# Two-block cross-attention units with trailing value products, and pooling projections ahead of the second block's self-attention

## The chip, the cores and the metric

The kernel runs on one core of a Trainium2 chip. Five engines work side by side on their own instruction queues: TensorE (PE, matrix products; its weight loads are shown as PEld), VectorE (DVE), ScalarE (ACT), GpSimd (POOL) and SyncE (SP, which here only issues transfers). An engine takes its queue in order and waits on semaphores for the others. Matrix products are written to PSUM, which has eight banks of 128 x 512 fp32 numbers; everything else lies in SBUF. The metric is device time in microseconds (us), median of several runs.

## The reference, cut to what matters

Two transformer blocks run one after the other on a sequence of 512 rows of width 1024. Only the second block is touched. It computes:

```
for l in range(2):
    hn = rms_norm(h, norm_mix_g[l])
    if l == 0: h = h + even_mixer(hn, ...)      # differential attention + pooling
    else:      h = h + odd_mixer(hn, ...)       # gated convolution
    h = h + cross_attention(rms_norm(h, norm_xattn_g[l]), mem_n, wq[l], wkv[l], wo[l])
    h = h + sq_relu_mlp(rms_norm(h, norm_mlp_g[l]), w1[l], w2[l])
```

`even_mixer` projects `hn` to q, k, v and u. Four heads of causal differential attention, with two softmaxes each, `softmax(q1 k1) - lam * softmax(q2 k2)`, go through v and a norm. Four groups of u are pooled over 2, 4, 8 and 16 rows and pass through a 128 x 128 matrix each. `cross_attention` has four heads of width 256 against 256 memory rows, with `softmax(q k / 16) v`, and then `@ wo`.

## The kernel before, in words

Activations are held transposed, features on partitions, rows of the sequence along the free dimension. Each is kept as a pair hi/lo of the reduced-precision type fp32r (`P0H`, `P0L`, `P1H`, `P1L`; `MH`, `ML` for the memory), and so is each weight (`whi`, `wlo`). A big product is three passes, hi*hi, lo*hi and hi*lo (`gemm_fm`, L315, passes L325 to L327; `gemm_tm`, L335, passes L350 to L352). A weight chunk is loaded by SP into `raw`, rounded to `whi` by ScalarE (L180) and its rest put into `wlo` by VectorE (L171, 128 x 1024). The projections of a chunk of 128 output columns are 8 steps of 3 passes, one `yield` after each step.

The attention products are plain fp32, which PE runs as two passes each. A unit is one block of 128 query rows of one head (self-attention: two score maps). `attention` (L511) steps through units and issues four things for each:

- `scores`: q times k into PSUM (L525), then on VectorE the maximum (L534, or L542 together with the bias) and its negation, and on ScalarE the exponential into a tile `Tb`.
- `norm`: VectorE divides by the sum (and combines the two maps, L174).
- `turn`: PE transposes the probabilities (L588), ScalarE copies them from PSUM to `PTb`.
- `values`: PE multiplies v by `PTb` (L613) into an output bank. The last unit of a head ends with `done_pair`.

In round i, the order is `norm(i-1)`, `values(i-2)`, `scores(i)`, a pause, `turn(i-1)`, a pause. `drive(main, fill, num, den)` (L365) runs `main`, the attention, up to a pause and then takes on average num/den steps from `fill`, which holds big products that don't depend on it. So the order on every engine is fixed when the program is built: `fill` is what PE does while a unit's softmax is under way.

In the even mixer, all four query projections stand ahead of the attention. `fill_E` (L1201) has the four pooling projections (`project`), their mixes (`mix`) and the keys and values of the first cross-attention (`kv`, L1237), at 132/49 steps per pause. `project(g)` is evacuated by VectorE into `UP`; GpSimd makes 1 to 4 additions; a `rest` that VectorE does later (`waiting`) finishes it. In `kv` a key step is three passes of 256 columns and a value step six.

`cross` (L1320) computes the queries of head 0 and then runs 16 units, four per head. Its `fill` has the queries of heads 1 to 3 and, in layer 0 only, the second layer's `kv`. The steps per pause are 5 in layer 0 and 9/4 in layer 1. Then `xattn_wo` follows (`mixed`, L1307), 8 gemms that each need all four heads.

From the even mixer on there are three `Tb` tiles, two `PTb`, two score banks (`SB`), one bank for transposes, two output banks and three banks for big products.

Of the kernel before, what the change touches and what calls it, by code (L numbers as in the profile page):

```python
# [5 lines left out]
F32 = mybir.dt.float32  # L6
F32R = mybir.dt.float32r
ACT = mybir.ActivationFunctionType
ALU = mybir.AluOpType
# [132 lines left out]
def lay_out(nc, A, plan, T):  # L142
# [172 lines left out]
    def gemm_fm(src, w, parts, evac, N=512, last=True, n0=0):  # L315
# [3 lines left out]
        for n, (b, t) in enumerate(parts):  # L319
# [11 lines left out]
            yield  # L331
# [179 lines left out]
    def attention(units, done_pair):  # L511
# [3 lines left out]
        def scores(u):  # L515
# [13 lines left out]
            for j, ((bank, _), p) in enumerate(zip(banks, prods)):  # L529
# [3 lines left out]
                if u["kind"] == "plain":  # L533
                    o = op(DV, lambda e, mx=mx, bank=bank: e.reduce_max(mx, bank[:, 0:kl], axis=AX), p, sfree)  # L534
                elif u["kind"] == "forget":
# [12 lines left out]
                else:  # L548
                    o = op(DV, ts(nm, mx, -1.0, None, ALU.mult), o)
                src = bank[:, 0:kl] if u["kind"] == "plain" else t[:, 0:kl]  # L550
                x = op(AC, act(t[:, 0:kl], src, ACT.Exp, bias=nm, accum_out=l), o,
                       tfree if u["kind"] == "plain" else None)
                if u["kind"] == "plain":
                    SB.give(bank, x)
# [599 lines left out]
    for i in range(4):  # L1154
        w = Weight(chunk("ab_w_in", 0, halves(0), halves(128 * i, 1)))
        run(gemm_fm(P0, w, parts8(), to_rows(0.125, qE[:, i, :], tok, ("q", i))))
# [43 lines left out]

    def fill_E():  # L1201
        def project(g):
            w = Weight(chunk("ab_w_in", 0, halves(0), halves(1536 + 128 * g, 1)))
            yield from gemm_fm(P0, w, parts8(), pool_evac(g))

        def mix(g):
            w = Weight(chunk("pool_w", g, halves(0, 1), halves(0, 1)))

            def evac(bank, p):
                t, free = TMP.take()  # L1210
                o = op(DV, ts(t, bank, gcol("ps", g), None, ALU.mult), p, free)
                split_into(P1, 4 + g, t, o, give=t)
                return o

            assert P1.tok[g] is not None
            yield from gemm_fm(P1, w, [(0, g)], evac)

        for g in range(4):
            for n, _ in enumerate(project(g)):
                if n == 3 and g:  # L1220
                    waiting.pop(g - 1)()
                yield
            if g:
                yield from mix(g - 1)
        keys = kv(0)
        for n in range(12):
            if n == 7:
                waiting.pop(3)()
            next(keys)
            yield  # L1230
        yield from mix(3)
        yield from keys

# [3 lines left out]
    def kv(l, before=None):  # L1237

        kvt = kvtok[l]
        for h in range(4):  # L1240
            while before and not all("T" in u for u in before[4 * h:4 * h + 4]):
                yield
            for i in (2 * h, 2 * h + 1):
# [6 lines left out]
                yield from gemm_fm(MEM, w, parts8(), evac, N=256)  # L1250
            while before and not all("over" in u for u in before[4 * h:4 * h + 4]):
                yield
# [6 lines left out]
    for h in range(4):  # L1259
        for i in range(4):  # L1260
# [3 lines left out]
                qk=[tok[("q", h)], tok[("k", h)]],  # L1264
# [19 lines left out]
    def even_main():  # L1284
        yield from attention(eun, head_done)
# [18 lines left out]
    drive(even_main(), fill_E(), 132, 49)  # L1304
# [15 lines left out]
    def cross(l, gname):  # L1320
# [10 lines left out]
        un = []  # L1331
        for h in range(4):
            for i in range(4):
                un.append(dict(
                    kind="plain", len=256, pair=h, nout=2, first=i == 0, last=i == 3,
                    qk=lambda h=h: [tok[2 * h], tok[2 * h + 1], kvt[("k", 2 * h)], kvt[("k", 2 * h + 1)]],
                    mm=[[(qX[:, 2 * h + d, 128 * i:128 * i + 128], KT[:, 2 * h + d, :]) for d in range(2)]],
                    vtok=[kvt[("v", 2 * h)], kvt[("v", 2 * h + 1)]],
                    outs=[(d, 0, 128, 128 * i,
                           [VM[:, j, 256 * h + 128 * d:256 * h + 128 * d + 128] for j in range(2)], 0)  # L1340
                          for d in range(2)]))

        def done(u, banks, p):
            fr = []
            for d in range(2):
                m = 2 * u["pair"] + d
                a = op(AC, act(P1.hi[:, m, :], banks[d], ACT.Copy), p)
                o = op(DV, sub(P1.lo[:, m, :], banks[d], P1.hi[:, m, :].bitcast(F32)), a)
                P1.tok[m] = [a, o]
                fr.append(o)  # L1350
            return fr

        def fill():
            for h in range(1, 4):
                yield from qs(h)
            if l == 0:
                yield from kv(1, un)

        if l == 0:
            drive(attention(un, done), fill(), 5, 1)  # L1360
# [331 lines left out]
```

How the kernel before makes its waits and increments, by code:

```python
    def dma(self, eng, fn, sem, val, *deps):  # L93
        self.op(eng, lambda e: fn(e).then_inc(sem, 16), *deps)
        return Landed(sem, val)
# [9 lines left out]
    def play(self, eng, e):  # L105
        seen = {}
        for o in self.of[eng]:
            need = {}
            for d in o.deps:
                v = need.get(id(d.sem), (0, None))[0]
                need[id(d.sem)] = (max(v, d.val), d.sem)
            for k, (v, s) in need.items():
                if seen.get(k, 0) < v:
                    e.wait_ge(s, v)
                    seen[k] = v
            ins = o.fn(e)
            if o.sig:
                ins.then_inc(o.sem, 1)
# [23 lines left out]
def lay_out(nc, A, plan, T):  # L142
# [1348 lines left out]
    d, o = diagonal(RC[:, 0:4], rstd(NS[:, 0:4], o, RC[:, 0:4]))  # L1491
    bank, free = SB.take()
    p = op(PE, lambda e: e.matmul(bank, ones, d, start=True, stop=True), o, free, c_ones)
    row = op(AC, act(RB[:, :], bank, ACT.Copy), p)
    for n, m in enumerate((0, 5, 1, 2, 6, 3, 7, 4)):
        if m > 4:
            o = op(PO, mult(X[:, m, :], X[:, m, :], RB[:, :]), row, gained[m])
        else:
            o = op(DV, stt(X[:, m, :], X[:, m, :], gcol("last", m), RB[:, :], ALU.mult, ALU.mult), row)
        Q.dma(SP, lambda e, m=m: e.dma_start(A["outT"][:, m, :], X[:, m, :]), T["s_o"], 16 * (n + 1), o)
    op(SP, lambda e: e.wait_ge(T["s_o"], 128))
    return Q, used
```

## Time and profile before

| | |
|---|---|
| median of 3 runs | 2375.24 us (2373.6 to 2375.85) |
| the profiled execution | 2375.47 us, of which the span of instructions 2373.7 |
| PE busy | 2323.9 us, 98% of the span |
| VectorE, ScalarE, GpSimd busy | 56%, 36%, 1% |
| mean granted PE clock | 0.996 |

The span is the time from the first instruction to the last. A matrix product is pipelined: its recorded time includes its way through the array, so the next one starts before it ends, and the pace is read from start to start. A wait is shown as idle time behind a row, with what ended it.

### The profile page before, as it was taken

The numbers are of one execution on the slowest core, as the hardware profiler recorded it, in microseconds if no ns is written. First come the engines' busy times: TensorE is split into PE (matmuls) and PEld (weight loads), VectorE is DVE, ScalarE is ACT, GpSimd is POOL, SyncE is SP. The second block draws the span as 40 slices with busy tenths as digits, with TensorE's granted clock in tenths as the row PEclk, the third lists the DMA queues.
The fourth block names the chain that finished last, engine by engine and source line by source line (L and its number), as shares of the span: only waits on it lengthen the run. The fifth ranks groups of instructions, "written<-read, shape, count | busy, mean of one in ns | idle before, by whom it ended". The sixth has DMA issues, their size and how long they took to land.

```text
span 2373.7 us, 28772 instructions
## 1 busy us (share of the span) xinstructions
PE 2323.9 (98%) x11510; PEld 1875.8 (79%) x11510; DVE 1324.4 (56%) x2470; ACT 858.4 (36%) x1483; POOL 23.3 (1%) x21
## 2 busy tenths in 40 slices
PE   8999999999999999989999999999999989999997
PEld 6787778878777787878798888888888878888886
DVE  5855565556656657486545544444755545444444
ACT  4334443433444334254333432232322334332232
POOL 1000000000000000010000000000000000000000
PEclk9999999999999999999999999999999999999998
DMA  4322223322322233223233322223233213223221
GB/s 164 105 74 86 77 74 99 103 81 85 98 71 77 78 103 112 76 90 116 89 97 108 98 90 97 98 90 97 89 98 98 80 36 98 95 92 98 97 90 54
DMA packets 65417, 217.00 MB, mean 91 GB/s; under 512 B 8415, under 2 KB 9695, under 8 KB 65156
## 3 DMA queue, kind: packets, MB, share of 16 engines
q1 hardware_dynamic: 65284, 215.16, 28.6%
q8 instruction: 91, 1.49, 0.2%
q14 instruction: 42, 0.34, 0.0%
HBM read 207.78 MB, written 2.11 MB: 88 GB/s over the span
## 4 chain that ended last, share of the span: by engine, by line
PE 95%; DVE 3%; ACT 1%; issue 0%; DMA 0%; DVEq 0%; SPq 0%; ACTq 0%
PE ps L325 27%; PE ps L327 26%; PE ps L326 26%; PE ps L525 3%; PE ps L613 3%; PE ps L588 2%; PE ps L350 2%; PE ps L351 1%; PE ps L352 1%; DVE t_wlo L171 1%; PE ps L414 1%; DVE t_P0L L174 0%; ACT t_Tb L180 0%; PE ps L868 0%; PE ps L870 0%
## 5 line engine op out<-in xcount | busy, mean ns | idle before, releaser
L325 PE MATMUL ps<-t_P0H,t_whi 128*128 128x512 f32 x1664 | 676.8, 407 | 8.7 <-DVE t_P0L L174 8.6
L327 PE MATMUL ps<-t_P0H,t_wlo 128*128 128x512 f32 x1664 | 656.7, 395 | 0.0
L326 PE MATMUL ps<-t_P0L,t_whi 128*128 128x512 f32 x1664 | 655.0, 394 | 0.0
L180 ACT ACTIVATE t_whi<-t_raw 128x1024 fp32r<-128x1024 f32 (+2 forms) x396 | 404.7, 1026 | 384.4 <-PE ps L327 328.5
L171 DVE TENSOR_TENSOR t_wlo<-t_raw,t_whi 128x1024 fp32r<-128x1024 f32 (+2 forms) x396 | 469.5, 1188 | 11.4 <-ACT t_whi L180 6.3
L325 PEld LDWEIGHTS ps<-t_P0H,t_whi 128*128 128x128 f32 x1664 | 313.6, 188 | 102.2 <-issue 24.8
L327 PEld LDWEIGHTS ps<-t_P0H,t_wlo 128*128 128x128 f32 x1664 | 312.9, 188 | 73.1
L326 PEld LDWEIGHTS ps<-t_P0L,t_whi 128*128 128x128 f32 x1664 | 313.6, 188 | 67.6 <-issue 2.2
L325 PE MATMUL ps<-t_P1H,t_whi 128*128 128x512 f32 x900 | 354.6, 394 | 0.7 <-DVE t_P1L L171 0.7
L327 PE MATMUL ps<-t_P1H,t_wlo 128*128 128x512 f32 x900 | 354.8, 394 | 0.0
L326 PE MATMUL ps<-t_P1L,t_whi 128*128 128x512 f32 x900 | 354.2, 394 | 0.0
L325 PEld LDWEIGHTS ps<-t_P1H,t_whi 128*128 128x128 f32 x900 | 169.5, 188 | 41.0 <-DVE t_P1L L171 1.6
L327 PEld LDWEIGHTS ps<-t_P1H,t_wlo 128*128 128x128 f32 x900 | 169.1, 188 | 39.2
L326 PEld LDWEIGHTS ps<-t_P1L,t_whi 128*128 128x128 f32 x900 | 169.2, 188 | 39.0
L168 DVE TENSOR_TENSOR t_X<-ps,t_X 128x512 f32<-128x512 f32 x128 | 88.5, 692 | 163.4 <-PE ps L327 163.4
L180 ACT ACTIVATE t_TMP<-t_TMP 128x512 f32<-128x512 f32 x89 | 56.4, 633 | 280.5 <-DVE t_TMP L174 229.2
L174 DVE SCALAR_TENSOR_TENSOR t_TMP<-ps,t_RB 128x512 f32<-128x512 f32 x64 | 44.3, 692 | 178.4 <-PE ps L327 178.3
L180 ACT ACTIVATE t_Tb<-t_Tb,t_ST 128x128 f32<-128x128 f32 (+3 forms) x128 | 67.5, 528 | 208.2 <-DVE t_ST L177 208.2
L174 DVE SCALAR_TENSOR_TENSOR t_X<-ps,t_X 128x512 f32<-128x512 f32 x48 | 33.2, 692 | 112.1 <-PE ps L327 112.1
L180 ACT ACTIVATE t_P0H<-t_X,t_gv 128x512 fp32r<-128x512 f32 x56 | 40.0, 724 | 148.3 <-DVE t_X L174 136.2
L180 ACT ACTIVATE t_PTb<-ps 128x256 f32<-128x256 f32 (+3 forms) x176 | 63.4, 397 | 65.8 <-PE ps L588 65.6
L180 ACT ACTIVATE t_P1H<-t_TMP 128x512 fp32r<-128x512 f32 x89 | 56.3, 632 | 70.8 <-DVE t_TMP L165 47.7
(235 smaller groups left out, 2495.5 us busy)
## 6 DMA issues: line engine op xcount, KB each, us to landing
t_raw<-in_wts SPq DMA_DIRECT2D x364, 512.0 KB, 3.5
t_raw<-in_wts SPq DMA_DIRECT2D x16, 384.0 KB, 3.0
t_raw<-in_wts SPq DMA_DIRECT2D x4, 520.0 KB, 6.3
t_X<-in_xT SPq DMA_DIRECT2D x4, 512.0 KB, 6.3
t_raw<-in_wts SPq DMA_DIRECT2D x8, 256.0 KB, 2.7
outT<-t_X SPq DMA_DIRECT2D x8, 256.0 KB, 2.3
t_TMX<-t_TMX SPq DMA_DIRECT2D x28, 64.0 KB, 2.0
t_TMP<-t_TMX SPq DMA_DIRECT2D x24, 64.0 KB, 2.0
```

The source lines that it names most:

```text
L168: return lambda e: e.tensor_tensor(o, a, b, ALU.add)
L171: return lambda e: e.tensor_tensor(o, a, b, ALU.subtract)
L174: return lambda e: e.scalar_tensor_tensor(out=o, in0=a, scalar=s, in1=b, op0=f, op1=g)
L180: return lambda e: e.activation(o, a, f, **k)
L325: e.matmul(bank[:, 0:N], wh, xh, start=first, stop=False)
L326: e.matmul(bank[:, 0:N], wh, xl, start=False, stop=False)
L327: return e.matmul(bank[:, 0:N], wl, xh, start=False, stop=end)
L350: e.matmul(out, xh, wh, start=k == 0, stop=False)
L351: e.matmul(out, xh, wl, start=False, stop=False)
L525: i = e.matmul(bank[:, 0:kl], l, r, start=n == 0, stop=n == len(mm) - 1)
L588: i = e.transpose(bank[:, 128 * j:128 * j + 128], t[:, 128 * j:128 * j + 128], ident[:, :])
L613: i = e.matmul(o, vs[j], pts[n][:, 128 * j:128 * j + 128], start=j == 0, stop=j == nk - 1)
```

## The change

Three things are changed.

1. Cross-attention gets loops of its own. A unit is now two blocks of 128 queries of a head, so there are 8 units in a layer. One `reduce_max` over a 128 x 2 x 256 view serves both blocks, there are two exponentials of 256 columns, one division over 512 columns, four transposes into one bank, and value products with 256 moving columns. The order of a round is `norm(i-1)`, `scores(i)`, a pause, `values(i-2)`, `turn(i-1)`, a pause. In layer 1, `fill` also starts the first two gemms of `xattn_wo` on the heads that are done (parts 0 to 5), with empty steps between; these two are ended behind the loop. The rate there is 13/3 in place of 9/4. `kv(1)` waits for two units of a head where it waited for four.
2. `attention` takes `late_values`, which the even mixer sets: `values(i-2)` stands behind the first pause, right ahead of `turn(i-1)`. The other callers keep their order.
3. In the even mixer, the four pooling projections and query 0 run ahead of the attention, and queries 1 to 3 go into `fill_E`, which now holds queries, mixes and `kv(0)`. A key step of `kv` is six passes (`every=2`). The rate is 92/49.

```
-            yield
+            if n % every == every - 1:
+                yield
...
         for i in range(n + 2):
             if 1 <= i <= n:
                 norm(units[i - 1])
-            if i >= 2:
+            if i >= 2 and not late_values:
                 values(units[i - 2])
             if i < n:
                 scores(units[i])
             yield
             flush()
+            if i >= 2 and late_values:
+                values(units[i - 2])
             if 1 <= i <= n:
                 turn(units[i - 1])
             yield
...
+    for g in range(4):
+        for n, _ in enumerate(project(g)):
+            if n == 3 and g:
+                waiting.pop(g - 1)()
+    run(queries(0))
+    waiting.pop(3)()
+
     def fill_E():
+        yield from queries(1)
+        for g in (0, 2):
+            yield from mix(g)
+            yield from mix(g + 1)
+            yield from queries(2 + g // 2)
+        yield from kv(0)
...
-    drive(even_main(), fill_E(), 132, 49)
+    drive(even_main(), fill_E(), 92, 49)
...
+        def values(u):
...
+                for d in range(2):
+                    o = held[h][d][0][:, 256 * n:256 * n + 256]
+                    for j in range(2):
+                        c = 256 * h + 128 * d
+                        i = e.matmul(o, VM[:, j, c:c + 128], pt[:, 256 * j:256 * j + 256], start=j == 0, stop=j == 1)
...
+            for m in range(2):
+                open_.append(wo(m))
+            for parts, rest in ((range(0, 4), 1), (range(4, 6), 3)):
+                for g in open_:
+                    for k in parts:
+                        assert P1.tok[k] is not None
+                        next(g)
+                        for _ in range(1 + rest):
+                            yield
...
-            drive(attention(un, done), fill(), 9, 4)
-        run(mixed("xattn_wo", l, halves(0), 1.0, gname, P1))
+            drive(main(), fill(), 13, 3)
+        for g in open_:
+            run(g)
+        for m in range(len(open_), 8):
+            run(wo(m))
```

On PE, in the middle of the even mixer's attention, the order before was this (`t_ident` marks transposes, `t_PTb` value products, `t_MH` and `t_ML` the fill of `kv`; an x3 stands for three alike):

```order
L588 MATMUL ps<-t_ident,t_Tb 128x128 x3
L325 MATMUL ps<-t_MH,t_whi 128x256
L326 MATMUL ps<-t_ML,t_whi 128x256
L327 MATMUL ps<-t_MH,t_wlo 128x256
L325 MATMUL ps<-t_MH,t_whi 128x256
L326 MATMUL ps<-t_ML,t_whi 128x256
L327 MATMUL ps<-t_MH,t_wlo 128x256
L325 MATMUL ps<-t_MH,t_whi 128x256
L326 MATMUL ps<-t_ML,t_whi 128x256
L327 MATMUL ps<-t_MH,t_wlo 128x256
L613 MATMUL ps<-t_PTb,t_E_82 128x128 x3
L525 MATMUL ps<-t_E_82 128x128 x2
```

The value products of a unit follow its transposes after one pause. In the changed program the same engine and place read:

```order
L526 MATMUL ps<-t_E_82 128x128 x2
L325 MATMUL ps<-t_MH,t_whi 128x256
L326 MATMUL ps<-t_ML,t_whi 128x256
L327 MATMUL ps<-t_MH,t_wlo 128x256
L325 MATMUL ps<-t_MH,t_whi 128x256
L326 MATMUL ps<-t_ML,t_whi 128x256
L327 MATMUL ps<-t_MH,t_wlo 128x256
L608 MATMUL ps<-t_PTb,t_E_82 128x128 x3
L583 MATMUL ps<-t_ident,t_Tb 128x128 x4
```

The value products (x3) now belong to a unit whose transposes stand a whole round earlier, with another unit's scores between. At the end of the second layer's cross-attention, PE had this before, up to the last row ahead of `xattn_wo` (`t_KT` marks scores):

```order
L613 MATMUL ps<-t_PTb,t_VM 128x128 x4
L525 MATMUL ps<-t_KT,t_E_82 128x256 x2
L588 MATMUL ps<-t_ident,t_Tb 128x128 x2
L613 MATMUL ps<-t_PTb,t_VM 128x128 x4
L525 MATMUL ps<-t_KT,t_E_82 128x256 x2
L588 MATMUL ps<-t_ident,t_Tb 128x128 x2
L613 MATMUL ps<-t_PTb,t_VM 128x128 x4
L588 MATMUL ps<-t_ident,t_Tb 128x128 x2
L613 MATMUL ps<-t_PTb,t_VM 128x128 x4
```

There was no fill left. The changed program has, near the same place:

```order
L1392 MATMUL ps<-t_PTb,t_VM 128x256 x4
L1368 MATMUL ps<-t_ident,t_Tb 128x128 x4
L325 MATMUL ps<-t_P1H,t_whi 128x512
L326 MATMUL ps<-t_P1L,t_whi 128x512
L327 MATMUL ps<-t_P1H,t_wlo 128x512
L325 MATMUL ps<-t_P1H,t_whi 128x512
L326 MATMUL ps<-t_P1L,t_whi 128x512
L327 MATMUL ps<-t_P1H,t_wlo 128x512
L1342 MATMUL ps<-t_KT,t_E_82 128x256 x4
```

The six passes between are two steps of `xattn_wo`. On VectorE, where the even mixer's attention begins, the rows before are the evacuation of query 3 (into `t_E_82`), a clearing of `UP` and the first unit's softmax (L542):

```order
L174 SCALAR_TENSOR_TENSOR t_E_82<-ps,t_RB 128x512
L1159 MEMSET t_UP 128x3x16
L542 ISA t_Tb,t_ST<-ps,t_E_82 128x128
L542 ISA t_ST 128x1
L177 TENSOR_SCALAR t_ST<-t_ST 128x1
```

and in the changed program:

```order
L165 TENSOR_TENSOR t_UP<-ps,t_RB 128x512
L171 TENSOR_TENSOR t_wlo<-t_raw,t_whi 128x128
L174 SCALAR_TENSOR_TENSOR t_E_82<-ps,t_RB 128x512
L174 SCALAR_TENSOR_TENSOR t_TMP<-t_UP 128x496
L165 TENSOR_TENSOR t_UP<-t_UP,t_ic 128x16
L171 TENSOR_TENSOR t_TMP<-t_UP 128x16
L541 ISA t_Tb,t_ST<-ps,t_E_82 128x128
```

Query 0 is evacuated right ahead of the first softmax, and the end of pooling group 3, which waits for GpSimd, stands between.

## Rows read from the trace of the kernel before

**Rows 1.** The page's first part: busy time of each engine and instructions.

```profile
PE 2323.9 (98%) x11510; PEld 1875.8 (79%) x11510; DVE 1324.4 (56%) x2470; ACT 858.4 (36%) x1483; POOL 23.3 (1%) x21
```

**Rows 2.** Stretches: length, busy per engine, PEclk (granted clock), DMA share, GB/s.

```profile
972.40:994.70 22.30, 22.30 (x98) 17.88 (x96) 8.50 (x10) 4.45 (x5) 0.00 (x0) 1.00 0.24 78
994.70:1037.00 42.30, 40.00 (x200) 29.01 (x199) 36.74 (x111) 19.89 (x49) 11.54 (x10) 1.00 0.23 71
1037.00:1089.00 52.00, 44.54 (x323) 38.37 (x324) 40.01 (x127) 26.56 (x59) 1.12 (x1) 0.97 0.30 93
...
1245.00:1282.00 37.00, 34.04 (x266) 32.44 (x265) 18.97 (x43) 13.73 (x29) 0.00 (x0) 1.00 0.35 112
...
1931.90:1955.20 23.30, 14.98 (x90) 12.63 (x89) 7.80 (x25) 5.67 (x18) 0.00 (x0) 0.93 0.00 1
```

**Rows 3.** PE's waits from 1037 to 1089: total us, times, longest.

```profile
PE ps L613 <- ACT t_PTb L180: 4.5, 4, 2.2
PE ps L588 <- DVE t_Tb L174: 3.5, 3, 2.5
```

**Rows 4.** PE's timeline in that stretch: start us, us, engine, line, [idle before <-releaser].

```profile
1056.19 1.13 PE L525 MATMUL ps<-t_E 64*128 64x512 f32 x4
...
1058.89 0.28 PE L326 MATMUL ps<-t_ML,t_whi 128*128 128x256 f32 x1
...
1059.73 0.28 PE L327 MATMUL ps<-t_MH,t_wlo 128*128 128x256 f32 x1
1062.20 1.15 PE L613 MATMUL ps<-t_PTb,t_E 128*128 128x128 f32 x6 [2.20 <-ACT t_PTb L180]
```

**Rows 5.** ScalarE's timeline in the same microseconds.

```profile
1058.27 0.73 ACT L180 ACTIVATE t_Tb<-t_Tb,t_ST 128x512 f32<-128x512 f32 x1 [2.78 <-DVE t_ST L177]
...
1059.79 1.99 ACT L180 ACTIVATE t_whi<-t_raw 128x1024 fp32r<-128x1024 f32 x2
1061.68 0.47 ACT L180 ACTIVATE t_PTb<-ps 128x384 f32<-128x384 f32 x1
```

**Rows 6.** VectorE's timeline in the same microseconds.

```profile
1059.61 2.48 DVE L171 TENSOR_TENSOR t_wlo<-t_raw,t_whi 128x1024 fp32r<-128x1024 f32 x2
...
1062.84 0.75 DVE L174 SCALAR_TENSOR_TENSOR t_Tb<-t_Tb,t_ST 128x512 f32<-128x512 f32 x1
```

**Rows 7.** PE's timeline, end of the second layer's cross-attention.

```profile
1931.97 1.10 PE L613 MATMUL ps<-t_PTb,t_VM 128*128 128x128 f32 x8
1932.91 1.03 PE L525 MATMUL ps<-t_KT,t_E 128*128 128x256 f32 x4
1933.77 0.38 PE L588 MATMUL ps<-t_ident,t_Tb 128*128 128x128 f32 x2
1935.51 1.16 PE L613 MATMUL ps<-t_PTb,t_VM 128*128 128x128 f32 x8 [1.36 <-ACT t_PTb L180]
...
1955.19 0.48 PE L325 MATMUL ps<-t_P1H,t_whi 128*128 128x512 f32 x1
```

**Rows 8.** ScalarE's timeline there.

```profile
1934.62 0.47 ACT L180 ACTIVATE t_Tb<-ps,t_ST 128x256 f32<-128x256 f32 x1 [2.76 <-DVE t_ST L177]
...
1935.09 0.37 ACT L180 ACTIVATE t_PTb<-ps 128x256 f32<-128x256 f32 x1
...
1940.31 1.09 ACT L180 ACTIVATE t_P1H<-ps 128x512 fp32r<-128x512 f32 x2 [1.25 <-PE ps L613]
```

**Rows 9.** VectorE's timeline there.

```profile
1940.94 1.29 DVE L171 TENSOR_TENSOR t_P1L<-ps,t_P1H 128x512 fp32r<-128x512 f32 x2 [1.57 <-ACT t_P1H L180]
```

**Rows 10.** PE's timeline where the first layer's cross-attention begins.

```profile
1172.68 1.13 PE L525 MATMUL ps<-t_KT,t_E 128*128 128x256 f32 x4 [0.78 <-DVE t_E L174]
```

**Rows 11.** VectorE by shape, 990 to 1101: times | busy us, mean ns | idle before.

```profile
L171 DVE TENSOR_TENSOR t_wlo<-t_raw,t_whi 128x1024 fp32r<-128x1024 f32 x16 | 20.2, 1271 | 0.4 <-ACT t_whi L180 0.4
...
L165 DVE TENSOR_TENSOR t_UP<-ps,t_RB 128x512 f32<-128x512 f32 x4 | 2.8, 688 | 1.2 <-PE ps L327 1.1
```

**Rows 12.** GpSimd's timeline: the additions of pooling group 3.

```profile
1032.37 5.75 POOL L168 TENSOR_TENSOR t_UP<-t_UP 128x512 f32<-128x512 f32 x4 [7.74 <-DVE t_UP L165]
```

More of the change, by code:

```diff
@@ L508, in residual, with attention @@
         return make
-    def attention(units, done_pair):
+    def attention(units, done_pair, late_values=False):
         st = {}
@@ L1199, in lay_out, with project, mix, evac @@
     c_ic = load(T["ic"][:, :], A["ic"], deps=[hrow])
-    def fill_E():
[L1202 to L1232, printed above, removed]
+    def project(g):
+        w = Weight(chunk("ab_w_in", 0, halves(0), halves(1536 + 128 * g, 1)))
+        yield from gemm_fm(P0, w, parts8(), pool_evac(g))
+    def mix(g):
+        w = Weight(chunk("pool_w", g, halves(0, 1), halves(0, 1)))
+        def evac(bank, p):
+            t, free = TMP.take()
+            o = op(DV, ts(t, bank, gcol("ps", g), None, ALU.mult), p, free)
+            split_into(P1, 4 + g, t, o, give=t)
+            return o
+        assert P1.tok[g] is not None
+        yield from gemm_fm(P1, w, [(0, g)], evac)
+    for g in range(4):
[4 more added lines that the diff above has]
+    waiting.pop(3)()
+    def fill_E():
+        yield from queries(1)
[4 more added lines that the diff above has]
+        yield from kv(0)
     KT, VM = T["KT"], T["VM"]
@@ L1240, in kv @@
         for h in range(4):
-            while before and not all("T" in u for u in before[4 * h:4 * h + 4]):
+            while before and not all("T" in u for u in before[2 * h:2 * h + 2]):
                 yield
@@ L1248, in evac @@
                     return kvt[("k", i)]
-                yield from gemm_fm(MEM, w, parts8(), evac, N=256)
-            while before and not all("over" in u for u in before[4 * h:4 * h + 4]):
+                yield from gemm_fm(MEM, w, parts8(), evac, N=256, every=2)
+            while before and not all("over" in u for u in before[2 * h:2 * h + 2]):
                 yield
@@ L1343, in done, with both @@
[L1343 to L1351, printed above, removed]
+        un = [dict(head=h, half=n) for h in range(4) for n in range(2)]
+        def both(ap):
+            return ap.rearrange("p (a b) -> p a b", a=2)
@@ new lines, in scores, with f @@
+        def scores(u):
+            h = u["head"]
+            bank, free = SB.take()
+            t, tfree = TB.take()
+            s, sfree = STT.take()
+            def f(e):
+                for a in range(2):
+                    q0 = 128 * (2 * u["half"] + a)
+                    for d in range(2):
+                        i = e.matmul(bank[:, 256 * a:256 * a + 256], qX[:, 2 * h + d, q0:q0 + 128],
+                                     KT[:, 2 * h + d, :], start=d == 0, stop=d == 1)
+                return i
+            p = op(PE, f, [tok[2 * h], tok[2 * h + 1], kvt[("k", 2 * h)], kvt[("k", 2 * h + 1)]], free)
+            o = op(DV, lambda e: e.reduce_max(s[:, 0:2], both(bank), axis=AX), p, sfree)
+            o = op(DV, ts(s[:, 2:4], s[:, 0:2], -1.0, None, ALU.mult), o)
+            u["exp"] = [op(AC, act(t[:, 256 * a:256 * a + 256], bank[:, 256 * a:256 * a + 256], ACT.Exp,
+                                   bias=s[:, 2 + a:3 + a], accum_out=s[:, 4 + a:5 + a]), o, tfree)
+                        for a in range(2)]
+            SB.give(bank, u["exp"])
+            u["t"], u["s"], u["T"] = t, s, True
@@ new lines, in main, with nxt @@
+        def main():
+            n = len(un)
+            for i in range(n + 2):
+                if 1 <= i <= n:
+                    norm(un[i - 1])
+                if i < n:
+                    scores(un[i])
+                yield
+                flush()
+                if i >= 2:
+                    values(un[i - 2])
+                if 1 <= i <= n:
+                    turn(un[i - 1])
+                yield
+        def nxt(m, o):
+            norm_tile(m, o, gname, P0, sqa)
+        ev = residual(1.0, nxt, P0)
@@ L1353, in fill, with wo @@
+        def wo(m):
+            w = Weight(chunk("xattn_wo", l, halves(0), halves(128 * m, 1)))
+            return gemm_fm(P1, w, parts8(), ev(m))
+        open_ = []
         def fill():
```

76 lines of the change are left out of this document (51 added, 25 removed).

## The prediction

> **What bounds the kernel now.** I read four views in this order. The page's first part shows PE busy for 2323.9 us [rows 1] of a span of 2373.7, so at most 50 us of waits can go anywhere, and the change adds or removes no big product. What it can win is idle PE time and, a little, the pace of small products. Second, the table of stretches [rows 2] tells where the idle time lies. While the even mixer's queries run, PE never waits: 96 passes take 22.3 us, 0.232 us a pass of 512 columns, 5.6 us a gemm of 24. In the attention behind it PE loses 42.3 - 40.0 = 2.3 us and then 52.0 - 44.5 = 7.5. At the end of the first cross-attention it loses 37.0 - 34.0 = 3.0, at the end of the second 23.3 - 15.0 = 8.3. These 21.1 us are in stages that the change touches. In two of the stretches the granted clock is under 1: 0.97 of 52 us and 0.93 of 23.3, each about 1.6 us lost at the lower level. Third, PE's waits [rows 3] say for what: value products wait for the `PTb` copy by ScalarE, transposes for `Tb` from VectorE. Fourth, the timelines show why.
>
> In the even mixer, scores of a 512-key unit start at 1056.19 and end by 1057.25 or so [rows 4]. ScalarE's copy of the unit before it is queued behind both exponentials of that new unit and behind two weight roundings, 1.99 us, and starts only at 1061.68 [rows 5]. PE had only some 18 narrow passes left to do by then, 0.12 us each (1058.89 to 1059.73 is seven steps), and stood 2.20 us. So a copy is ready about 5 us behind the next unit's scores, and PE comes to it after 2.8.
>
> At the end of the second cross-attention there is no fill. One round from value product to value product lasts 1935.51 - 1931.97 = 3.54 us, of which 0.94 is values, 0.86 scores and 0.24 two transposes (two of eight passes in 0.94) [rows 7]. Here too the copy stands behind the next unit's exponential: 1935.09 behind 1934.62 [rows 8].
>
> **The even mixer, minus 8.9 us.** What it loses now: 9.8 us idle, 1.6 for the clock, and about 0.15 us for PE to start again behind each of some ten waits: 12.9. The work itself only moves: a pooling gemm leaves the loop and a query gemm enters for each, and one gemm of 5.6 us more stands in front.
>
> After the change, the pause is 92/49 = 1.88 steps of 0.7 us, so 1.3 us, all through the loop; before it was 1.9 us with wide steps and 0.95 with narrow ones. With the trailing order, what lies between the scores of a unit and the values that wait for the copy behind its exponentials is three pauses, one group of values with transposes, and one of scores: 3.9 + 0.85 + 0.65 = 5.4 us against the 5 us needed. So the waits for `PTb` go, even with two roundings in the way. The transposes are late next: the last division of that 512-key unit ended at 1062.84 + 0.75 = 1063.6 [rows 6], 6.35 us behind its scores, with 2.48 us of weight rests in between. The new distance is 5.4 + 0.65 = 6.05, so 0.3 us is short where two rests meet one of these units, some four times.
>
> VectorE is what can spoil this. From 994.7 to 1089 it was busy 36.7 + 40.0 = 76.7 us [rows 2]. Out of the loop go four evacuations of 0.69, four weight rests of 1.27 [rows 11] and the four last parts of pooling, at least another 0.69 each; in come three evacuations and three rests. That is 10.6 - 5.9 = 4.7 us less, 72 us. PE's work in that time is 94.3 - 11.4 lost - 5.6 = 77.3 us. VectorE is then at 93%, in a fixed order. The cost of that is between nothing and all 9.8 us of idle time that the loop has now; I take 3 us, nearer to the side where the distances cover, since the load is evenly spread.
>
> In front, each group's end waits for GpSimd while VectorE holds its queue: weight rests, evacuations and the next softmax are behind it. The longest is group 3, 5.75 us of additions [rows 12], against the 5.6 us gemm of query 0 that covers it; VectorE was busy for 8.5 of 22.3 us there [rows 2], so the 7 us of work that comes in fits. What is new is a wait: the first scores need query 0, which PE has just ended. The trace has the same place in cross-attention: 0.78 us idle for the evacuation [rows 10], about 1.0 with the restart. Before, query 0 was three gemms old. So 12.9 - 3.0 - 1.0 = 8.9.
>
> **The first cross-attention, minus 3.3 us.** Fill was there, but empty steps left two rounds bare, 3.0 us and two restarts. With 5 steps in a pause, 48 query steps and 64 of the next layer's keys and values last beyond the 20 pauses (100 steps), and the order has no round without fill. Scores to transposes are then three pauses of 3.5 us. The wait of 0.78 at its start stays.
>
> **The second cross-attention, minus 7.9 us.** From 1931.97 to 1955.19 PE spent 23.2 us on 7 groups of values, 6 of scores and 6 of transposes: 7 x 0.94 + 6 x 0.86 + 6 x 0.24 = 13.2, so 10.0 us are lost, the lower clock among them. Now 12 steps of `xattn_wo` stand between the last units, and the 0.7 us that each takes is work that PE has to do anyway. New waits come with them. Parts 4 and 5 need the halves of head 2, for which ScalarE takes 1.09 for two [rows 8] and VectorE 1.29 for two [rows 9]; the first is ready some 1.4 us behind the values, while transposes and one step cover 1.1. I take 0.7 for both parts. Behind the last values nothing covers head 3: part 6 waits those 1.4 us in full. Before, 18 passes of `xattn_wo`, 4 us, stood there and PE did not wait. So 10.0 - 0.7 - 1.4 = 7.9.
>
> **Wider value products, minus 1.3 us.** Two passes of 128 columns take 2 x 0.94/8 = 0.235 us, one of 256 columns 0.86/4 = 0.215 in the scores [rows 7]. There are 256 of the narrow passes in both layers, so 128 x 0.02 = 2.6 us if the values behave as the scores do, and none if the 0.94 has a restart in it. I take the middle. Two blocks in one maximum and one division save VectorE instructions, but VectorE is no limit there: no cover, no gain.
>
> **The sum.** 8.9 + 3.3 + 7.9 + 1.3 = 21.4 us from the profiled execution's own 2375.47, so 2354 us. The median shown, 2375.24, differs from it by 0.2, which changes nothing. All other stages keep their instructions.
>
> **The rivals.** (a) VectorE becomes the limit of the even mixer's loop, and the idle time moves but stays: 9.8 in place of 3 us, 6.8 us more, 2361. For it speak the 93% and the waits for `Tb`; against it that VectorE was at 77% in the stretch that lost most, 40.0 of 52.
>
> (b) The lower clock comes at the waits that are left. It has come twice, in the two stretches that lost most, and each time cost 1.6 us [rows 2]; if it comes as often, 3.2 us more, 2357. The Trainium skill, "TensorE: Matmul & The Clock Gate", section "A second HAM failure mode: psum-queue depth-cycling", says that frequent short idles between groups of matmuls can make the clock fall and rise again and again. By that rule shorter waits need not be a cure; the trace so far had it only in the two stretches with most idle time, 7.5 and 8.3 us, while the first part of the loop, with 2.3, kept 1.00 [rows 2].
>
> (c) The other side, slower: the units run in lockstep. A unit takes two of three `Tb` tiles, and one of them is free only behind its transposes. If the next unit's softmax had to wait for these, each unit would show its whole chain: 1056.19 to 1063.6, then transposes, copy and values, 0.5 + 0.5 + 1.0, so 9.4 us; 16 units make 150 us in place of 94.3, near 2410. It decides from the point where transposes of unit i-1 stand behind the scores of unit i+1. The order has them ahead, so little speaks for it.
>
> (d) The change does not do what it says: each copy is still behind the next exponentials and roundings, and the pauses of 1.3 us in the even mixer, shorter than the 1.9 of wide steps before, lose elsewhere what the order wins; the early `xattn_wo` steps wait for the heads in place of the units. Then 2371 to 2376.
>
> **How the numbers follow.** The forecast has 0.66, (a) 0.20, (b) 0.06, (c) 0.03, (d) 0.05. The lower end takes no loss in the loop (3.0), the full 1.3 more for wide products and no wait for head 2 or its like (2.1): 2354 - 6.4, so 2347. The upper end takes (a), no gain from width, and one fall of the clock: 6.8 + 1.3 + 1.6, and 2 us for more at the heads of the second cross-attention, so 2366. Outside lie (c), (d) and little more. A measurement of this kernel can tell about 0.2%, 4.8 us, from no change: faster is under 2370.5. All of the first three cases are: 0.92; within 0.05, most of (d); slower 0.03.
>
> **What would show it.** After the change, waits of value products for `PTb` in the even mixer and in both cross-attentions should be near 1 us in all, where the second part of the even loop alone had 4.5 [rows 3]; transposes should wait 1 to 4 us for `Tb`; two new waits should stand at the first even scores and at the `xattn_wo` step behind the last value products, and the last 24 us before `xattn_wo` should have no row of PE with over 2 us idle. A VectorE over 95% busy through the even loop with PE idle there by some 10 us would make it (a). A bare gap at each pooling gemm in front would show that GpSimd's additions were not covered, which I priced at nothing.

## The result, and the profile after

The changed kernel took 2355.68 us, median of 4 runs (2355.14 to 2356.94), against 2375.2 before (2373.6 to 2375.85): ratio 0.992, 95% interval 0.9902 to 0.9937. The profiled execution took 2355.40, its span 2353.6. One run of kernel e2 below took 13100.59 us, a slow one, and its ratio leaves it out.

Where the 20 us came from is read by cutting both spans at the same products: a stage ends where PE starts the row-sum products of the norm behind it (`t_P1H` by `t_ones`), and the even mixer begins at the last flip product in front of it. The three touched stages of the kernel before, with their length, each engine's busy time, and PEclk behind the last bracket:

```profile
968.46:1165.75 197.29, 186.70 (x1060) 153.10 (x1059) 132.10 (x312) 83.58 (x157) 12.66 (x10) 0.99 0.29 90
1165.75:1337.06 171.31, 167.56 (x995) 147.61 (x994) 88.52 (x154) 63.64 (x108) 0.00 (x0) 1.00 0.32 99
1871.63:2005.31 133.68, 124.57 (x612) 103.09 (x610) 64.72 (x122) 47.90 (x92) 0.00 (x0) 0.99 0.19 64
```

and those of the changed kernel:

```profile
969.86:1158.09 188.23, 183.71 (x1060) 151.32 (x1059) 128.40 (x312) 83.27 (x157) 13.37 (x10) 1.00 0.29 95
1158.09:1325.39 167.30, 166.29 (x932) 145.26 (x930) 85.36 (x122) 62.52 (x100) 0.00 (x0) 1.00 0.31 101
1859.94:1985.27 125.33, 121.88 (x547) 99.61 (x546) 61.16 (x90) 46.43 (x84) 0.00 (x0) 1.00 0.21 68
```

| stage | before | after | change | of it PE idle | of it PE busy |
|---|---|---|---|---|---|
| all before the even mixer | 968.46 | 969.86 | +1.40 | | |
| even mixer | 197.29 | 188.23 | -9.06 | -6.07 | -2.99 |
| first cross-attention | 171.31 | 167.30 | -4.01 | -2.74 | -1.27 |
| second cross-attention | 133.68 | 125.33 | -8.35 | -5.66 | -2.69 |

The three stages gave 21.4 us; the rest of the span, 902.9 us before and after, did not move. The 1.4 us given back at the start are no work of the change: PE's first product begins at 8.29 us before and at 9.69 after, and over all the kernels below that stretch came out anywhere from 968.5 to 970.6, with the same code in it. The busy time that went is in part the lower clock (0.99 in two stages before, 1.00 in all three now) and in part the wider products (0.4 us in each cross-attention, e6). The rest is put down to products that take longer right behind a wait; no run shows that by itself.

PE as a whole answers to [rows 1]:

```profile
PE 2317.3 (98%) x11382; PEld 1868.7 (79%) x11382; DVE 1313.7 (56%) x2406; ACT 855.3 (36%) x1467; POOL 23.5 (1%) x21
```

The waits of [rows 3] are gone from the value products. PE's waits from 994 to 1110 in the changed kernel (total us, times, longest):

```profile
PE ps L583 <- DVE t_Tb L174: 2.8, 3, 1.9
PE ps L325 <- DVE t_wlo L171: 0.9, 2, 0.5
PE ps L526 <- DVE t_E L174: 0.8, 1, 0.8
```

No row names `PTb`, here or in either cross-attention. The kernel before waited for it in all three stages, here the even mixer (two rows) and the first and the second cross-attention:

```profile
PE ps L613 <- ACT t_PTb L180: 5.1, 5, 2.2
PE ps L588 <- DVE t_Tb L174: 3.9, 4, 2.5
PE ps L613 <- ACT t_PTb L180: 2.7, 2, 1.4
PE ps L613 <- ACT t_PTb L180: 8.3, 6, 2.4
```

What answers to [rows 4] is PE around the longest wait that is left, the 1.9 us for `Tb`:

```profile
1053.62 1.13 PE L526 MATMUL ps<-t_E 64*128 64x512 f32 x4
...
1059.74 0.83 PE L608 MATMUL ps<-t_PTb,t_E 128*128 128x128 f32 x6
1062.48 0.66 PE L583 MATMUL ps<-t_ident,t_Tb 128*128 128x128 f32 x4 [1.92 <-DVE t_Tb L174]
```

ScalarE there, for [rows 5]:

```profile
1056.50 0.72 ACT L180 ACTIVATE t_Tb<-t_Tb,t_ST 128x512 f32<-128x512 f32 x1
...
1057.22 0.47 ACT L180 ACTIVATE t_PTb<-ps 128x384 f32<-128x384 f32 x1
1057.90 2.01 ACT L180 ACTIVATE t_whi<-t_raw 128x1024 fp32r<-128x1024 f32 x2 [0.21 <-PE ps L353]
```

and VectorE, for [rows 6]:

```profile
1057.90 0.76 DVE L165 TENSOR_TENSOR t_VM<-ps,t_MRC 128x256 f32<-128x256 f32 x2 [1.44 <-PE ps L353]
1058.57 2.35 DVE L171 TENSOR_TENSOR t_wlo<-t_raw,t_whi 128x1024 fp32r<-128x1024 f32 x2
...
1061.67 0.75 DVE L174 SCALAR_TENSOR_TENSOR t_Tb<-t_Tb,t_ST 128x512 f32<-128x512 f32 x1
```

The copy of `PTb` is still queued behind the exponentials (1057.22 behind 1056.50). Two things are different. The value product that wants it stands later: it starts 6.1 us behind the scores of the next unit (1059.74 behind 1053.62), where PE had come to it after 3.8 before (1060.0 behind 1056.19 [rows 4]). And the copy itself comes sooner, 3.6 us behind these scores where it was 5.5 (1061.68 behind 1056.19 [rows 4, 5]), because the two weight roundings that stood in front of it now stand behind it. The transposes are late now, as forecast: VectorE spends 2.35 us on two weight rests, and the division ends at 1062.42.

At the end of the second cross-attention, PE's timeline, for [rows 7]:

```profile
1921.94 2.00 PE L1342 MATMUL ps<-t_KT,t_E 128*128 128x256 f32 x8 [0.77 <-DVE t_E L174]
...
1925.17 1.89 PE L1392 MATMUL ps<-t_PTb,t_VM 128*128 128x256 f32 x8
1926.89 0.60 PE L1368 MATMUL ps<-t_ident,t_Tb 128*128 128x128 f32 x4
...
1928.72 1.89 PE L1342 MATMUL ps<-t_KT,t_E 128*128 128x256 f32 x8
...
1931.84 1.89 PE L1392 MATMUL ps<-t_PTb,t_VM 128*128 128x256 f32 x8
...
1935.15 0.50 PE L325 MATMUL ps<-t_P1H,t_whi 128*128 128x512 f32 x1 [0.29 <-DVE t_P1L L171]
...
1936.65 1.89 PE L1392 MATMUL ps<-t_PTb,t_VM 128*128 128x256 f32 x8
...
1940.20 1.89 PE L1392 MATMUL ps<-t_PTb,t_VM 128*128 128x256 f32 x8
```

No value product waits. The idle time of the stage is 3.4 us: 1.7 at scores for their queries, and 1.7 at `xattn_wo` for its input, as PE's waits in it say:

```profile
PE ps L1342 <- DVE t_E L174: 1.7, 3, 0.8
PE ps L325 <- DVE t_P1L L171: 1.7, 2, 1.4
```

### The profile page after: what moved, and what is told of

Read it like the earlier page. It is cut to its first block, busy times and chain, and to the rows that moved or that the text cites. A ratio compares the mean times of both kernels' runs of the same rounds, so it can differ in the third digit from the quotient of the medians.

```text
span 2353.6 us, 28454 instructions
## 1 busy us (share of the span) xinstructions
PE 2317.3 (98%) x11382; PEld 1868.7 (79%) x11382; DVE 1313.7 (56%) x2406; ACT 855.3 (36%) x1467; POOL 23.5 (1%) x21
## 3 DMA queue, kind: packets, MB, share of 16 engines
q8 instruction: 90, 1.47, 0.3%
## 4 chain that ended last, share of the span: by engine, by line
PE 96%; DVE 3%; ACT 0%; DMA 0%; issue 0%; DVEq 0%; SPq 0%; ACTq 0%
PE ps L325 27%; PE ps L327 27%; PE ps L326 27%; PE ps L526 2%; PE ps L608 2%; PE ps L351 2%; PE ps L352 2%; PE ps L583 2%; PE ps L353 2%; PE ps L1342 1%; PE ps L1392 1%; PE ps L415 1%; DVE t_wlo L171 1%; DVE t_P0L L174 0%; PE ps L865 0%; PE ps L866 0%
## 5 line engine op out<-in xcount | busy, mean ns | idle before, releaser
L180 ACT ACTIVATE t_whi<-t_raw 128x1024 fp32r<-128x1024 f32 (+3 forms) x396 | 404.7, 1026 | 383.7 <-PE ps L327 324.1
L171 DVE TENSOR_TENSOR t_wlo<-t_raw,t_whi 128x1024 fp32r<-128x1024 f32 (+3 forms) x396 | 468.3, 1186 | 11.7 <-ACT t_whi L180 6.7
```

The costliest lines, as they stand in the source:

```text
L171: return lambda e: e.tensor_tensor(o, a, b, ALU.subtract)
L180: return lambda e: e.activation(o, a, f, **k)
```

## The experiments

Each was profiled and timed beside the kernel before. The table has the lengths of the touched stages from each kernel's profile, us, cut as above. "Falls" are the stretches in them with the granted clock at its lower level, 1.2 in place of 2.4 GHz. All are of one length but e1's in the even mixer, which is twice as long and counted as two.

| kernel | even mixer | first cross | second cross | falls | median | ratio, 95% |
|---|---|---|---|---|---|---|
| before | 197.29 | 171.31 | 133.68 | 1 even, 1 second | 2375.2 | |
| after | 188.23 | 167.30 | 125.33 | none | 2355.68 | 0.9902 to 0.9937 |
| e1 | 193.82 | 171.25 | 133.90 | 2 even, 1 second | 2372.58 | 0.9977 to 0.9995 |
| e2 | 191.71 | 171.30 | 132.21 | none | 2372.97 | 0.9974 to 0.9992 |
| e3 | 198.91 | 167.34 | 125.24 | 2 even | 2365.71 | 0.9946 to 0.9973 |
| e4 | 189.72 | 167.35 | 126.74 | 1 even | 2356.77 | 0.9907 to 0.9935 |
| e5 | 189.87 | 165.64 | 121.12 | 1 even | 2351.27 | 0.9879 to 0.9909 |
| e6 | 188.18 | 167.73 | 125.78 | none | 2356.36 | 0.9901 to 0.9928 |
| e7 | 191.92 | 167.28 | 125.29 | none | 2359.29 | 0.9915 to 0.994 |
| e8 | 189.70 | 166.79 | 129.46 | 1 even, 1 second | 2360.12 | 0.9917 to 0.9942 |
| e9 | 188.19 | 167.67 | 125.06 | none | 2354.79 | 0.9896 to 0.9923 |
| e10 | 185.96 | 165.64 | 121.12 | none | 2347.28 | 0.986 to 0.9891 |
| e11 | 188.17 | 167.30 | 125.25 | none | 2355.42 | 0.9898 to 0.9925 |

Stages are compared rather than medians, since they repeat to 0.1 us with the same code, or 0.2 with a fall in them. e1 to e4 were timed on one chip, e5 to e7 on another, e8 to e11 on a third, and the kernel before took 2376.71, 2376.97 and 2376.71 us beside them; the ratios are against these.

**e1: the trailing order alone, in the even mixer of the kernel before.**

```
-            if i >= 2:
+            if i >= 2 and not late_values:
                 values(units[i - 2])
             ...
             yield
             flush()
+            if i >= 2 and late_values:
+                values(units[i - 2])
```

> The kernel before with one edit: in the even mixer the value products of unit i-2 stand behind the first pause. Theory one (the trailing order lets the copy to PTb pass the next unit's exponentials): the value products' waits of 5.1 us in the even loop fall under 1, restarts and the lower clock there go with them; 6 us less than before, 2369. Theory two (the even mixer's gain comes from taking pooling work off VectorE and from even pauses): at most 1 us less, 2374 to 2376.

**e2: the changed kernel's front of the even mixer (pooling gemms first, queries, the rate and the wide key steps), with the old order of the products and the old cross-attention.** The edit shown is against the changed kernel.

```
-        yield from attention(eun, head_done, late_values=True)
+        yield from attention(eun, head_done)
```

> The kernel before with the pooling projections in front of the loop, queries in the fill, 92/49 and wide key steps, but with the old order of the value products and the old cross-attention. Theory one: between a unit's transposes and its values lies one pause of 1.3 us, from the next scores' end to the values 2.9 us where 5 are needed, so the 384 and 512-key units wait some 2 us each; no gain, 2374 to 2382. Theory two: VectorE is relieved and pauses are even, 5 to 8 us less, 2368.

**e3: the new cross-attention alone, on the kernel before.** Its edit is the cross-attention part of the change; the first lines:

```
-        un = []
-        for h in range(4):
-            for i in range(4):
-                un.append(dict(
...
+        un = [dict(head=h, half=n) for h in range(4) for n in range(2)]
...
```

> The kernel before with the new cross-attention loops alone (both layers). If the parts add up: 4.0 us in the first and 8.4 in the second cross-attention, 12.4 less, 2363. If the even mixer's part and this one hang together (weights rounded at other moments, the clock), the sum with the even mixer's 9.1 us misses the 20 of the whole change by over 3 us.

e3 is the plain part: it took 4.0 and 8.4 us off the two cross-attentions, all that they lose in the change, and left the even mixer alone but for a second fall. For the even mixer neither half does it by itself, and both do something. The code of the kernel before took 197.29 with one fall and 198.91 with two (e3), so some 195.7 with none, an estimate. Against e3, which had as many falls, e1 is 5.1 shorter; e2, with none, is 4.0 shorter than 195.7; both together 7.5. PE's waits from 994 to 1110 in e1:

```profile
PE ps L588 <- DVE t_Tb L174: 4.0, 3, 2.5
PE ps L325 <- DVE t_P1L L171: 1.7, 1, 1.7
...
```

and in e2:

```profile
PE ps L614 <- ACT t_PTb L180: 2.3, 4, 0.9
PE ps L589 <- DVE t_Tb L174: 2.1, 2, 1.9
...
```

The order alone removes the waits for `PTb` and keeps those for `Tb`; the front alone cuts `PTb` from 5.1 to 2.3 and `Tb` from 3.9 to 2.1. That the order alone carries the even mixer, and that the front brings nothing, are both refuted.

**e4: the changed kernel without the early steps of `xattn_wo` between the last units.**

```
             if l == 0:
                 yield from kv(1, un)
-                return
-            for _ in range(3):
-                yield
-            for m in range(2):
-                open_.append(wo(m))
-            ...
```

> The changed kernel without the early steps of xattn_wo in the second cross-attention: its last four units then run with no fill. Theory three (my prediction's): the steps of xattn_wo are the cover, and what they cover is lost again; of 8.4 us some 5 or more come back, 2360 or over. Theory four (the order and the units of two blocks carry it, since 1.7 us of values and 1.7 us of scores lie between a product and its use): by hand 1.5 us at the values of unit 6 and 0.8 at those of unit 7 come, the 1.4 behind the last values and 0.3 for head 2 go, so 0.6 us more, 2356 to 2357.

The second cross-attention grew from 125.33 to 126.74 us, by 1.4: those steps are not what covers its end. PE's timeline there:

```profile
1923.66 1.99 PE L1342 MATMUL ps<-t_KT,t_E 128*128 128x256 f32 x8 [1.47 <-DVE t_E L174]
...
1933.40 1.99 PE L1392 MATMUL ps<-t_PTb,t_VM 128*128 128x256 f32 x8 [1.69 <-DVE t_P1L L171]
...
1936.52 1.99 PE L1392 MATMUL ps<-t_PTb,t_VM 128*128 128x256 f32 x8 [0.69 <-ACT t_PTb L180]
```

With nothing at all between the units, only 0.69 us go to `PTb`; the other two waits shown are for a query (1.47) and for the output bank of head 2 (1.69).

**e8: e4, with the value product ahead of the next scores again, in two-block units.**

```
+                if i >= 2:
+                    values(un[i - 2])
                 if i < n:
                     scores(un[i])
                 yield
                 flush()
-                if i >= 2:
-                    values(un[i - 2])
```

> The run without early xattn_wo steps (whose second cross-attention stage took 126.7 us), with one more edit in both cross-attentions: value products of unit i-2 stand ahead of the scores of unit i again, as in the kernel before, still with units of two blocks. Theory five (the trailing order is what removed the loss): the copy is behind the next exponentials again, 3.1 us from the end of the scores where transposes cover 0.4; two or three bare rounds wait 2.7 each, 5 to 8 us more in that stage, 132 to 134. Theory six (fewer, larger units are what removed it): under 2 us more, below 129.

**e9: the opposite: the changed kernel's even mixer, and the old cross-attention of sixteen one-block units with the trailing order.** The edit shown is against the cross-attention of the kernel before; layer 1 has the same one.

```
-            drive(attention(un, done), fill(), 5, 1)
+            drive(attention(un, done, late_values=True), fill(), 5, 1)
```

> The changed kernel's even mixer with the old cross-attention of 16 one-block units and no early xattn_wo steps, and the trailing order in it. Theory five: by rows of before a unit's softmax needs 1.85 us behind its scores where 2.98 lie between, and its copy 1.75 where 2.04 do, so bare rounds cost nothing but the ends of heads: the second cross-attention's stage takes 125 to 128 us, where before it took 133.7. Theory six: it stays at 131 to 134.

e8 took 129.46 us in the second cross-attention, with one fall, between its two theories (132 or more, and under 129). Its PE stood at the bare rounds, those without fill, again:

```profile
1926.90 3.68 PE L1392 MATMUL ps<-t_PTb,t_VM 128*128 128x256 f32 x8 [2.09 <-ACT t_PTb L180]
...
1935.02 1.97 PE L1392 MATMUL ps<-t_PTb,t_VM 128*128 128x256 f32 x8 [2.28 <-ACT t_PTb L180]
```

while e9, without wide products, without the two-block units and without early `xattn_wo` steps, took 125.06, no more than the changed kernel:

```profile
1920.21 1.03 PE L526 MATMUL ps<-t_KT,t_E 128*128 128x256 f32 x4
1921.08 1.05 PE L614 MATMUL ps<-t_PTb,t_VM 128*128 128x128 f32 x8
1921.97 0.38 PE L589 MATMUL ps<-t_ident,t_Tb 128*128 128x128 f32 x2
1922.19 1.03 PE L526 MATMUL ps<-t_KT,t_E 128*128 128x256 f32 x4
```

A bare round is 1922.19 - 1920.21 = 1.98 us, where it was 3.54 [rows 7]. So the trailing order is enough for the second cross-attention: alone it brought the old units from 133.68 to 125.06. Larger units also help, but less: under the old order they brought it from 133.68 to 129.46, one fall in each. Under the trailing order they add nothing: against the changed kernel e9 is 0.3 us better in the second cross-attention and 0.4 worse in the first, and with no early `xattn_wo` steps in either, two-block units (e4, 126.74) are 1.7 slower than one-block ones (e9).

What the order is worth thus depends on the units: 8.6 us for units of one block and 2.7 for units of two (129.46 in e8 against 126.74 in e4), with a fall in the slower one both times. In the first cross-attention, where there is fill, either does it alone: 171.31 before, 167.67 in e9, 166.79 in e8.

**e6: the changed kernel with the value products cut to 128 columns again.**

```
-                    for j in range(2):
-                        ...matmul(o, ..., pt[:, 256 * j:256 * j + 256], ...)
+                    for a in range(2):
+                        for j in range(2):
+                            ...matmul(o[:, 128 * a:128 * a + 128], ..., pt[:, 256 * j + 128 * a:256 * j + 128 * a + 128], ...)
```

> The changed kernel with the value products of cross-attention cut back to 128 moving columns (twice as many passes, same order). The prediction's term: 1.3 us more, between 0 and 2.6. If the narrow pass is held by its weight load and not by its columns: 2.6 or more. If the pass takes its columns alone: nothing that can be measured.

The stages grew by 0.43 and 0.45 us: width is worth 0.9 us here.

**e7: the changed kernel with one VectorE product of 128x512 more per unit of the even mixer.**

```
+            if late_values and i < n:
+                xt, xfree = TMP.take()
+                xo = op(DV, mult(xt, RB[:, :], RB[:, :]), N.row, xfree)
+                TMP.give(xt, xo)
```

> The changed kernel with one more VectorE product of 128x512 for each of the 16 units of the even loop, about 0.69 us each, 11 us in all, into a scratch tile that nobody reads. If VectorE is as near its limit there as the prediction's 93% says: 72 + 11 us of work in 77, so 6 to 9 us more, 2362 to 2365. If the loop is held by the distance of products from their use and VectorE has room: under 2 us more.

In the loop, the changed kernel's engines stood so (length, PE, PEld, DVE, ACT):

```profile
1002.60:1086.00 83.40, 79.66 (x526) 64.47 (x527) 69.00 (x224) 45.33 (x106) 1.31 (x2) 1.00 0.31 101
```

VectorE is busy for 69.0 of 83.4 us, 83%. In e7 it is 75.49 in the same window; its products by shape (times, busy us, mean ns, idle before):

```profile
L165 DVE TENSOR_TENSOR t_TMP<-t_RB 128x512 f32<-128x512 f32 x16 | 11.0, 685 | 0.0
```

Of 11.0 us of added work the stage shows 188.23 to 191.92, 3.7 us; the waits for `Tb` rise from 2.8 to 3.7 and for weight rests from 0.9 to 2.5. This is neither a bound (6 us or more) nor free room (under 2): VectorE has room in the mean and is late at single places.

**e5: the waits that were left, covered: two steps of fill ahead of the first scores of each stage, a third `xattn_wo` gemm opened early and ended behind the last values.** The three empty steps ahead of the early gemms go, and weights are prepared sooner behind the loop; these lines are not shown.

```
+    ahead_E = fill_E()
+    for _ in range(2):
+        next(ahead_E)
-    drive(even_main(), fill_E(), 92, 49)
+    drive(even_main(), ahead_E, 90, 49)
     ...
-            for m in range(2):
+            for m in range(3):
                 open_.append(wo(m))
     ...
+        for g in open_[2:]:
+            for _ in range(2):
+                next(g)
```

> The changed kernel with its new waits covered: two steps of the fill run ahead of the first scores in the even mixer and in both cross-attentions, three gemms of xattn_wo are begun early in place of two, none of the three empty steps stands ahead of them, and two of their steps are kept for behind the last values. If the waits named in the trace after are all that is left there: 1.2 at the first even scores, 1.06 at the start of each cross-attention, 1.06 at the scores of unit 6, 1.7 at the xattn_wo steps, 6 us less, 2350. If a wait that is covered only moves to the next one in line: 2354 to 2356.

Both cross-attentions lost what was left: 165.64 and 121.12, with 120.85 us of the second busy. The even mixer got none. PE's waits from 994 to 1110:

```profile
PE ps L608 <- ACT t_PTb L180: 3.6, 2, 2.1
PE ps L583 <- DVE t_Tb L174: 1.1, 2, 0.9
```

The wait for `PTb` is back, and ScalarE's timeline tells why:

```profile
1013.12 0.63 ACT L180 ACTIVATE t_P1H<-t_TMP 128x512 fp32r<-128x512 f32 x1
...
1015.24 0.63 ACT L180 ACTIVATE t_P1H<-t_TMP 128x512 fp32r<-128x512 f32 x1 [1.29 <-DVE t_TMP L177]
1015.78 1.04 ACT L180 ACTIVATE t_whi<-t_raw 128x1024 fp32r<-128x1024 f32 x1
1016.72 0.36 ACT L180 ACTIVATE t_PTb<-ps 128x256 f32<-128x256 f32 x1
```

Two steps of shift put two mixings of pooled rows into one pause. Each ends in a copy on ScalarE whose input comes from VectorE; the second waited 1.29 us for it, and the copy of `PTb` is queued behind both and a weight rounding.

**e10: e5 with the second mixing moved behind four steps of the next query.**

```
-            yield from mix(g + 1)
-            yield from queries(2 + g // 2)
+            q = queries(2 + g // 2)
+            for n, _ in enumerate(q):
+                yield
+                if n == 3:
+                    yield from mix(g + 1)
```

> The covered version with one more edit: in the even mixer's fill the four mixes no longer stand in pairs but four query steps apart. In the covered version two mixes in one pause had put two waits of 1.6 and 2.1 us for PTb there. If those come from ScalarE and VectorE handing the pair of mixes back and forth: they go, and the even stage takes 186 to 188 us without a fall of the clock (189.9 with one in the covered version), 2348 in all. If they come from the two steps of fill ahead of the first scores: they stay, 2350 to 2351.

The even mixer fell to 185.96 us, and the waits from 960 to 1110 to these:

```profile
PE ps L325 <- DVE t_wlo L171: 1.0, 1, 1.0
PE ps L583 <- DVE t_Tb L174: 0.9, 1, 0.9
PE ps L526 <- DVE t_ST L541: 0.5, 1, 0.5
```

At 2347.28 us it beats both kernels: 8.1 us less than the changed one beside it on the same chip (2355.42).

**e11: the changed kernel again, beside e8 to e10.** No edit.

> The changed kernel once more, beside the other three on the same chip: 2355 to 2358; every theory says the same.

It repeats: 188.17, 167.30 and 125.25.

## Why the prediction was right, and where its reasons were not

The forecast was 2354.0 in a range of 2347 to 2366; it came out at 2355.68. The three stages gave 21.4 us, as much as the sum; the 20.1 between the two profiled executions are less by the 1.4 us at the start, which the change doesn't touch. That the sum fits to 0.1 us is luck: two terms came out higher, width lower, and the changed kernel was profiled without a fall. Term by term:

- **Even mixer, 8.9: measured 9.06.** The size was right, and so was the remainder: 3.7 us in the loop (2.8 for `Tb`, 0.9 for weight rests) where 3 were taken, and 0.8 idle at the first scores where 1.0 with the restart was. The 3 us were a choice between nothing and 9.8, so part of this is luck. The working took the distances of the trailing order as the cause and held that the work in front "only moves". e1 and e2 show otherwise: each half alone is worth 5.1 and 4.0 us, 7.5 together when falls are taken out. e2 changes the place of the gemms, the rate and the width of key steps at once and about halves both waits; which of them does it is not shown. A relief of VectorE is not what does it in the share of time: VectorE was busy for 76.7 of 94.3 us, 81% of the loop, before [rows 2] and is for 83% now. The 0.15 us for a restart named no row, and no run isolates it.
- **The 0.3 us short, four times.** It came three times, with 0.24, 0.69 and 1.92 us, and only the longest at a 512-key unit: there the rests stood behind an evacuation that itself waited 1.44 us for PE. A distance taken from mean pauses has the right sign and not the size; it is the worst alignment that counts.
- **VectorE at 93%.** Measured 83% of the loop: 69.0 us in 83.4, where 72 in 77.3 were forecast. The working let four weight rests leave the loop and three come in; from the first scores to the last value product there are 13 rests of 128x1024 before and 14 after, since weights are prepared ahead of their gemm. Rival (a) did not come; by e7 it would have begun to count soon, at a third of a microsecond for each microsecond added.
- **First cross-attention, 3.3 and a part of the width: 4.01.** Without the 0.4 for width that is 3.6. The bare rounds are gone and the 0.8 at its start stays, as forecast; e8 and e9 show that the old order and the old units each would have done as well there.
- **Second cross-attention, 7.9 and the other part: 8.35. The size was right, the cover named for it was wrong.** The prediction put "12 steps of `xattn_wo`" between the last units as what removes the 10.0. They are worth 1.4 (e4). Without them, and without the two-block units, the trailing order alone brings 125.06 us (e9). The number did not depend on which cover it was: it was the time lost before, less the new waits. One round of other products between a copy and its reader, 1.98 us, is near enough to the copy's lateness. The waits at `xattn_wo` were 1.4 for head 3, as forecast, and 0.3 for head 2 where 0.7 was taken; one that was not forecast, 0.77 at the scores of the second-last unit for a query just ended, fills the gap.
- **Width, 1.3: mis-sized, 0.9.** It lies inside the bounds of 0 to 2.6. The 0.94 of [rows 7] was too long a pace for narrow passes: in e9 the same eight take 0.89 without a wait (1921.08 to 1921.97), and with that the term comes to 1.0.
- **Rivals.** (b), the lower clock: no fall in the touched stages of the changed kernel in two profiles of two, but one in the same even mixer in e4 and e8. It may come without a profile: one run of four at each timing of the changed kernel had a mean granted clock of 0.996 where the others had 0.997, and took 1.5 and 1.8 us more than the median of these. So it is a scatter of 1.5 us that the same order can have or not. The Trainium skill, "TensorE: Matmul & The Clock Gate", section "A second HAM failure mode: psum-queue depth-cycling", has frequent short idles as the cause; that fits with e3, which kept all the old waits of the even mixer and had two falls, but the same waits to the tenth went with a fall and without one (below), so the waits alone do not settle it. (c), lockstep: no sign of it, units overlap in every timeline. (d): refuted, the waits for `PTb` went altogether.

What stays open: how e2's front works, and whether the halves of the even mixer overlap. By stages less 1.6 us a fall, an estimate, they do (5.1 + 4.0 against 7.5). By medians, falls included, they do not: e1 and e2 took 4.1 and 3.7 us less than the kernel before beside them, while e4, timed with them, took 19.9 less, of which e3 has 11.0, so 8.9 are left against 7.8.

## What to carry to other kernels

When an in-order engine copies a result out of PSUM for PE, and its queue holds the next unit's work first, the reader should trail by a round; in the second cross-attention that order alone, with the old small units, brought all that the change did (133.68 to 125.06), and with it bigger units, wider products and extra fill could each be left out at a cost of 1.4 us or less. Look for what is queued in front of the copy, not at the copy: in e5 other copies put there went with waits of 3.6 us, and in e10 moving one of them ended these. Split a change whose parts all point at one wait before crediting any of them: the sum was right to 0.1 us here while a cover that it named was worth 1.4 of 8.4.

## What the runs showed of the hardware

The lower granted clock comes or stays away in one and the same code. The even mixer of the changed kernel's order took 188.23, 188.17, 188.18 and 188.19 us in four profiles without a fall and 189.72 and 189.70 in two with one. In e4 the stage's waits are the same to the tenth as in the changed kernel (2.8, 0.9 and 0.8), and yet the stretch from 1042 to 1090 was granted less; e4:

```profile
1042.00:1090.00 48.00, 46.09 (x354) 41.43 (x353) 34.94 (x111) 25.19 (x55) 0.00 (x0) 0.96 0.31 105
```

and the changed kernel, run again (e11), in the same stretch:

```profile
1042.00:1090.00 48.00, 46.08 (x366) 41.55 (x366) 36.30 (x114) 26.39 (x56) 0.00 (x0) 1.00 0.33 110
```

In the same 46.1 us of busy time PE got through 354 instructions in one and 366 in the other. A fall cost about 1.5 us there, and 1.5 to 1.7 in the old second cross-attention (132.21 without one in e2, 133.68 and 133.90 with one). Differences below that between single profiles have to be read beside the granted clock.

What PE did before is alike in all of them. In the thirteen profiles each of the ten stretches at the lower level in the touched stages begins within a wait of PE of 1.7 to 2.5 us or at most 1.5 us behind it: in e4 behind the 1.92 us that end at 1062.64. Eleven other waits of 1.7 to 2.6 us passed without one, among them the same 1.92 us in e11. e10, whose longest wait in these stages is 1.0 us, has none.
